# Other PSUM banks for the gathered rows and gates of a routed expert layer, and an earlier copy of the gates

## What is computed

```python
scores = sigmoid(xt @ router_w)                       # 256 tokens, 16 experts in 4 groups of 4
best_group = argmax(sum of the top 2 of scores + bias in each group)
expert_idx = the 2 best experts inside the best group
gate = scores[expert_idx] / sum(scores[expert_idx])
y[token] = sum over its 2 experts of gate * (silu(x @ w_gate[e]) * (x @ w_up[e])) @ w_down[e]
```

## Time and profile before

| what | value |
|---|---|
| three runs | 1366.31, 1368.42, 1367.08 us (median 1367.08) |
| profiled execution, its own time | 1365.09 us |
| its span (first to last instruction) | 1363.3 us |
| mean granted TensorE clock | 0.993 of full speed |
| TensorE matmul / VectorE / ScalarE / GpSimd busy | 95% / 69% / 52% / 7% of the span |
| DMA | 258.09 MB, mean 189 GB/s |

### The profile page before, as it was taken

How to read it: one execution, slowest core, us unless ns; L and a number is a source line. 1 busy time by engine, 2 the same in 40 slices (tenths; PEclk the granted TensorE clock), 3 DMA queues, 4 the chain that set the end, 5 groups by cost and what they waited for, 6 DMA issues and landing times.

```text
span 1363.3 us, 18226 instructions
## 1 busy us (share of the span) xinstructions
PE 1300.8 (95%) x7375; PEld 723.7 (53%) x7384; DVE 938.8 (69%) x1132; ACT 712.5 (52%) x760; POOL 95.0 (7%) x56
## 2 busy tenths in 40 slices
PE   6999999989999989999999999999989989999996
PEld 4686555446654445555557556444445555644443
DVE  5686776877764586464658576766867666678586
ACT  5466565345543364353456446555635673756462
POOL 0000000000000012000024002000004000300000
PEclk9999999999999999999999999999999999999999
DMA  9474434645655655564720235787936403569692
GB/s 319 136 248 157 152 124 155 224 170 186 211 206 189 240 189 198 172 236 159 249 96 1 74 135 166 260 286 254 365 128 231 171 1 124 186 197 328 215 342 91
DMA packets 152652, 258.09 MB, mean 189 GB/s; under 512 B 8881, under 2 KB 81532, under 8 KB 152572
## 3 DMA queue, kind: packets, MB, share of 16 engines
q1 hardware_dynamic: 152572, 256.97, 56.1%
HBM read 255.88 MB, written 1.07 MB: 188 GB/s over the span
## 4 chain that ended last, share of the span: by engine, by line
PE 81%; DVE 8%; DMA 4%; ACT 3%; issue 2%; DVEq 1%; POOL 1%; SPq 0%; ACTq 0%; POOLq 0%
PE ps L1215 13%; PE ps L1031 12%; PE ps L749 11%; PE ps L730 8%; PE ps L1033 6%; PE ps L1054 6%; PE ps L1294 6%; DVE w_ring L1923 4%; PE ps L767 3%; PE ps L991 2%; DMA w_ring<-in_exp_w_up 2%; PE ps L1271 1%; ACT w_hi L1489 1%; PE ps L694 1%; PE ps L1151 1%
## 5 line engine op out<-in xcount | busy, mean ns | idle before, releaser
L1923 DVE SCALAR_TENSOR_TENSOR w_ring<-w_ring,w_hi 128x2048 f16<-128x2048 f32 (+2 forms) x206 | 464.6, 2267 | 158.0 <-ACT w_hi L1489 156.8
L1489 ACT ACTIVATE w_hi<-w_ring 128x2048 f16<-128x2048 f32 (+2 forms) x206 | 381.6, 1864 | 225.1 <-PE ps L1054 50.9
L1031 PE MATMUL ps<-actT,w_hi 128*128 128x512 f16 x640 | 209.0, 380 | 0.7 <-issue 0.7
L1033 PE MATMUL ps<-actT,w_ring 128*128 128x256 f16 x640 | 174.8, 273 | 0.0
L749 PE MATMUL ps<-w_hi,actT 128*128 128x512 f16 x448 | 135.9, 379 | 2.9 <-DVE w_ring L1923 2.9
L1489 ACT ACTIVATE arena<-ps 128x256 f16<-128x256 f32 (+7 forms) x85 | 59.4, 709 | 143.9 <-PE ps L1033 77.1
L1215 PE MATMUL ps<-w_hi,arena 128*128 128x512 f16 x432 | 134.3, 379 | 0.0
L1215 PE MATMUL ps<-w_ring,arena 128*128 128x512 f16 x352 | 133.4, 379 | 0.0
L730 PE MATMUL ps<-w_hi,actT 128*128 128x512 f16 (+2 forms) x384 | 112.9, 371 | 2.8 <-DVE actT L1928 2.8
L1031 PEld LDWEIGHTS ps<-actT,w_hi 128*128 128x128 f16 x640 | 62.8, 98 | 77.4 <-issue 2.4
L1215 PE MATMUL ps<-arena 128*128 128x512 f16 x272 | 84.5, 379 | 3.8 <-DVE arena L2708 3.8
(11 more groups left out here) (430 smaller groups left out, 1934.2 us busy)
## 6 DMA issues: line engine op xcount, KB each, us to landing
w_ring<-in_dil_w_in SPq DMA_DIRECT2D x36, 1024.0 KB, 5.2
w_ring<-in_w_ff SPq DMA_DIRECT2D x32, 1024.0 KB, 5.1
w_ring<-in_exp_w_gate SPq DMA_DIRECT2D x64, 512.0 KB, 4.4
w_ring<-in_exp_w_up SPq DMA_DIRECT2D x64, 512.0 KB, 5.5
w_ring<-in_exp_w_down SPq DMA_DIRECT2D x32, 1024.0 KB, 5.7
w_ring<-in_w_in SPq DMA_DIRECT2D x24, 1024.0 KB, 5.1
w_ring<-in_sb_w_in SPq DMA_DIRECT2D x12, 1024.0 KB, 5.9
w_ring<-in_w_branch SPq DMA_DIRECT2D x8, 1024.0 KB, 5.0
```

The costliest lines, as they stand in the source:

```text
L1031: pe.matmul(ps[:, bank + c, :], w_h[:, k, cols], aT[:, kk, :], start=(kk == 0), stop=False, skip_group_check=True)
L1033: ins = pe.matmul(ps[:, bank + c, 0:S], w_l[:, k, cols], aT[:, kk, 0:S], start=False, stop=(kk == KD - 1), skip_group_check=True)
L1489: return act.activation(dst, src, ACT.Copy, scale=scale)
L1923: dve.scalar_tensor_tensor(out=lo16(h)[:, 0:kn * c], in0=w_ring[:, h % RING, 0:kn * c], scalar=W_POW, in1=hi16(h)[:, 0:kn * c], op0=ALU.mu ...
```

## The change

The six gathers use banks 7, 5, 6, 4, 7, 6 instead of 5, 7, 6, 4, 5, 7. The gates go to bank 5 instead of 6, and TensorE makes them before gather 4 instead of after it. VectorE copies them before split 8 instead of between `gathered(4)` and `gathered(5)`, and signals the copy, which is a new count in `route_dve` (11 a layer instead of 10); the drain behind it moves into pair 1, ahead of `slot_tokens`. TensorE waits, before `gate_up(1, 0, 1)`, for that copy instead of for VectorE's `gathered(5)`, and has a new wait for ScalarE's `gathered(5)` before `gate_up(1, 1, 0)`. TensorE's wait for ScalarE's `gathered(0)`, before gather 4, becomes one for `gathered(1)`, before the gates.

```diff
-GATHER_BANKS = (5, 7, 6, 4, 5, 7)
-ROUTE_PE = {"counts": 1, "rows": (2, 3, 4, 5, 6, 8), "gates": 7, "tokens": 9}
-ROUTE_DVE = {"best": 1, "groups": 2, "slots": 3, "rows": 4, "tokens": 10}
+GATHER_BANKS = (7, 5, 6, 4, 7, 6)
+ROUTE_PE = {"counts": 1, "rows": (2, 3, 4, 5, 7, 8), "gates": 6, "tokens": 9}
+ROUTE_DVE = {"best": 1, "groups": 2, "slots": 3, "rows": 4, "gates": 8, "tokens": 11}
...
 (TensorE, gather_gates)
-                            ins = pe.matmul(ps[:, 6, 4 * c:4 * c + 4], slot_of[:, t, c * P:(c + 1) * P],
+                            ins = pe.matmul(ps[:, 5, 4 * c:4 * c + 4], slot_of[:, t, c * P:(c + 1) * P],
...
 (TensorE, pair)
                     else:
                         gate_up(j, 0, 1, True)
                         if by_slots(j - 1):
                             to_tokens(j - 1)
+                        if j == 1:
+                            gathered(5)
                         gate_up(j, 1, 0)
...
                         gather(2)
                         gather(3)
-                        gathered(0)
+                        gathered(1)
+                        gather_gates()
                         gather(4)
                         gathered(2)
-                        gather_gates()
                         gather(5)
                         gathered(3)
                         gate_up(1, 0, 0)
-                        pe.wait_ge(sig("route_dve"), 10 * layer + ROUTE_DVE["rows"] + 5)
+                        pe.wait_ge(sig("route_dve"), 11 * layer + ROUTE_DVE["gates"])
                         return
...
 (VectorE, pair)
                         for h in range(3):
+                            if h == 2:
+                                dve.wait_ge(sig("route_pe"), 9 * layer + ROUTE_PE["gates"])
+                                dve.tensor_copy(r_few, ps[:, 5, 0:12]).then_inc(sig("route_dve"), 1)
                             if h:
                                 next_split(6 + h, j)
                             gathered(2 * h)
-                            if h == 2:
-                                dve.wait_ge(sig("route_pe"), 9 * layer + ROUTE_PE["gates"])
-                                dve.tensor_copy(r_few, ps[:, 6, 0:12])
-                                dve.drain()
                             gathered(2 * h + 1)
                     else:
                         if j == 1:
+                            dve.drain()
                             slot_tokens()
```

More of the change, by code:

```diff
@@ L581, in experts @@
                         if j == 1:
-                            sp.wait_ge(sig("route_dve"), 10 * layer + ROUTE_DVE["groups"])
+                            sp.wait_ge(sig("route_dve"), 11 * layer + ROUTE_DVE["groups"])
                             group_load("T")
@@ L1302, in counts @@
                 def counts():
-                    pe.wait_ge(sig("route_dve"), 10 * layer + ROUTE_DVE["best"])
+                    pe.wait_ge(sig("route_dve"), 11 * layer + ROUTE_DVE["best"])
                     g = [r_best[:, 4 * t:4 * t + 4] for t in range(T)]
@@ L1356, in pair @@
                         gate_up(j, 1, 1, True, (1,))
-                        pe.wait_ge(sig("route_dve"), 10 * layer + ROUTE_DVE["groups"])
+                        pe.wait_ge(sig("route_dve"), 11 * layer + ROUTE_DVE["groups"])
                         empty(3)
@@ L1378, in pair @@
                     if j == 0:
-                        pe.wait_ge(sig("route_dve"), 10 * layer + ROUTE_DVE["slots"])
+                        pe.wait_ge(sig("route_dve"), 11 * layer + ROUTE_DVE["slots"])
                         gather(0)
@@ L1391, in pair @@
                         gate_up(1, 0, 0)
-                        pe.wait_ge(sig("route_dve"), 10 * layer + ROUTE_DVE["rows"] + 5)
+                        pe.wait_ge(sig("route_dve"), 11 * layer + ROUTE_DVE["gates"])
                         return
                     if j == 1:
-                        pe.wait_ge(sig("route_dve"), 10 * layer + ROUTE_DVE["tokens"])
+                        pe.wait_ge(sig("route_dve"), 11 * layer + ROUTE_DVE["tokens"])
                     if few(j + 1):
@@ L1830, in gathered @@
                     if q >= 2:
-                        act.wait_ge(sig("route_dve"), 10 * layer + ROUTE_DVE["rows"] + q - 2)
+                        act.wait_ge(sig("route_dve"), 11 * layer + ROUTE_DVE["rows"] + q - 2)
                     for i in range(4):
```

## The result

The changed kernel takes **1360.2 us**, the median of 6 runs (1358.6 to 1361.5), and the kernel before, on the same chip, 1366.9 us (6 runs, 1365.9 to 1368.4). The ratio is 0.9949, with a 95% interval from 0.9940 to 0.9959, so it is faster by 0.5%. The forecast was 1363.0 with a range from 1361.3 to 1365.6: the sign was right, but the gain of 6.6 us lies outside the range, and 4.1 us were forecast. The profiled execution took 1358.78 us around a span of 1356.9, 6.3 less than the one of before (1365.09); its mean granted clock is 0.995 of full speed.

What follows compares the result with a forecast made beforehand. TensorE, busy 95% of the span, was taken to bound the kernel. Removing waits of 1.97 and 2.16 us gave -4.13, from a median of 1367.08 to 1362.95, stated as 1363.0 us, range 1361.3 to 1365.6.

Steps and rivals of the forecast that it cites:

- The two waits: TensorE's waits for VectorE's `gathered(5)` before `gate_up(1, 0, 1)` go: 1.97 us in layer 0, 2.16 in layer 1.
- split 8's end: Sign on VectorE: with the copy ahead of it, split 8 still ends near 843.
- silu: Sign on ScalarE: silu of pair 1 comes 1.97 us earlier, at 847.7.
- the first load: Sign on SyncE: its first load after the DMA's pause follows TensorE and moves from 847.27 to 845.3.
- The bounds of the copy: VectorE's copy of the gates beside GpSimd takes between 0.15 and 2.85 us; 0.15 was taken.
- the hold that hid the copy: Split 8 on VectorE is held until after GpSimd's end anyway, hiding 0.2 us of copy in front of it.
- A: DMA takes the gain back: TensorE's load wait near 889 grows 2 us; 1365.1 or 1367.1 us, chance 0.13.
- B: The copy's signal comes 3.7 us later than read, so TensorE waits for it at 842; 1367.1 us, chance 0.03.
- C: Half 9, behind the copy on VectorE, becomes TensorE's wait at 850; at worst 3.6 us a layer, 1374.2, chance 0.02.
- wait for `gathered(5)` of ScalarE: New TensorE wait before `gate_up(1, 1, 0)` costs zero, with 6.6 us to spare.
- rival D: Earlier products add or lose a half-clock stretch, as around 1005 us, of 1.7 us: 1364.7 or 1361.3; chance 0.10.
- It stayed 1.00 around the wait that goes: TensorE's granted clock stays at full speed around the removed wait, unlike the 0.85 and 0.81 after 1005 us.

Runs made afterwards that it cites:

- experiments 9: Kernel before with 8 products of zeros in each of TensorE's two waits for VectorE's gathered rows, TensorE not moved: 1364.7 us, ratio 0.9980.
- experiment 13: Kernel before with zeros in both waits for gathered rows and twice the zeros ahead of the stick-breaking projection: 1364.6 us, ratio 0.9983.
- 15: Kernel before with 8 products of zeros in layer 0's wait alone: 1366.6 us, ratio 1.0001.
- 16: Kernel before with 8 products of zeros in layer 1's wait alone: 1365.9 us, ratio 0.9997.
- 2: Kernel before with the whole change in layer 0 alone: 1363.3 us, ratio 0.9976.
- 3: Kernel before with the whole change in layer 1 alone: 1363.9 us, ratio 0.9975.

## Why the prediction was right in sign and wrong in size

**The two waits: right.** 1.97 and 2.16 us were forecast, 1.99 and 2.18 are gone from the stages. Also as forecast are the copy at 838.15 (forecast 838.5), split 8's end at 842.6 (near 843), silu at 847.5 (847.7) and the first load at 845.1 (845.3). These times carry the small difference of 0.2 us by which this execution is earlier.

**The bounds of the copy: the lower one held.** 0.16 us beside GpSimd, against bounds of 0.15 and 2.85. The Trainium skill (SBUF — State Buffer, Who interferes with whom) has it that a VectorE instruction with at most one input in SBUF, outside the modes that use two ports, doesn't contend with GpSimd; the row agrees for one that reads PSUM. Split 8 behind it still took 4.36 us instead of 2.28, with the hold that hid the copy.

**Rivals A, B and C: none came.** A needed the wait at 889 to grow by 2 us; it shrank from 1.31 to 1.00. B and C needed waits at 842 and 850; there are none. (B as written mixes two numbers: a signal 3.7 us later only begins to cost, and the full 1367.1 needs one 5.6 us later, 844.33 less 838.7.) TensorE has no wait for `gathered(5)` of ScalarE either.

**The failed step is rival D, the granted clock.** Its price was right: 1.7 us a stretch, measured as 1.68 to 1.69. Its place in the sum was wrong, in two ways.
- "It stayed 1.00 around the wait that goes" was read from one profile and taken as a property of the kernel. In half of the profiles with that wait of layer 1 idle, a stretch does follow it, and the one at 1005, which I treated as belonging to its own place, comes only in a part of the executions.
- I then gave D a chance of 0.10 and split it evenly, "half for either side". Nothing spoke for an even split: the change takes two idle stretches of about 2 us out of TensorE's stream and adds none, and at these two places the profiles without them show none. The sum lacked a third term beside -1.97 and -2.16. By the counts it is -1.9, which would have given 1367.08 - 4.13 - 1.9 = 1361.1 us; by the runs it is -2.4 to -2.7.

The price of a TensorE wait was counted as its length; here it was its length and some 0.6 of it again (2.4 to 2.7 on 4.17). By the same step the range was too narrow at its lower end: one stretch lost was the most that it allowed.

**What is shown and what is not.** Shown: without moving or removing any work, filling both waits takes away 2.7 and 2.2 us (experiments 9 and 13), and removing them instead takes away their length more. Shown in profiles, with few counts: at the projection and behind layer 1's wait the half-clock stretches are absent from every profile without the full idle wait ahead of them; elsewhere, as at 994 in experiment 13, they are not. Only argued: that such stretches are the extra; the clocks of all runs account for 1.6 +- 0.5 of 2.7 +- 0.4. Open: why a stretch comes in one execution and not in the next of the same kernel; why layer 0's wait, 160 us ahead of the projection, matters there; and why filling one wait alone (15, 16) brought nothing, while removing one alone (2, 3) brought 1.6 and 1.2 us more than its length. No kernel of these settles that.

## What to carry to other kernels

A short wait of TensorE in a dense stream costs its length and, in part of the executions, a stretch of half clock behind it or, as the counts here suggest, later: here 4.2 us of waits cost 6.6 to 6.9. Read the granted clock from several profiles of the same kernel before you call it constant, and price a wait that goes with both terms. Where a wait can't go, products of zeros in it can give back the second term (2.2 to 2.7 us here, with both waits filled; nothing measurable with one), but only where TensorE sets the pace: where other engines do, full clock comes back as a longer wait.

## What the runs showed that I had not expected

- A wait of 2.0 us can be enough, and once one of 1.79 was (experiment 13). In the third profile of before, two products behind a wait of 2.01 us run at full speed (2.4 GHz) and the following ones at half (1.2 GHz), for 1.69 us of loss; before the wait the stream was dense.
- It isn't the same in each execution. Three profiles of one kernel gave none, one and two stretches at these two places. It differs ahead of the changed code too: five of the eighteen profiles have stretches at 270 or 512 us or both, none at 302, and start layer 0's first gather at 822.0 to 822.5; the other thirteen start it at 819.3 to 820.9. In these five the wait of 3.0 us that ends at 302 is followed by full clock, so a longer wait isn't always followed by half. Of the kernel before, the 24 runs with the lowest clocks (0.990 and 0.991) took 1368.3 us on average and the other 86 1366.5, so part of the spread between its runs goes with such stretches.
- Half clock can be free. In the stick-breaking stage removing it moved 1.46 us from slow products into a wait (0.44 to 1.90).
